# Interleaving two attention groups in one unit order, with the query rotations and norm spreads as side steps between the units

## The reference, cut to what matters

```python
# A: latent attention, causal, one rotated key shared by the heads
q_nope = rmsnorm(q[..., :64], g_qn);  q_rope = rope(rmsnorm(q[..., 64:], g_qr), pos)
s = (q_nope @ k_nope.T + q_rope @ k_rope.T) * scale          # p, o as usual
# B: sliding windows (128,1), (512,4), (2048,16), merged by their softmax denominators
s = (qs @ ks.T) * 64**-0.5                                    # with the windows' mask
# new tokens: the same two, against 16 pages of 128 cached latents (A)
# and the last rows of a window buffer (B), for each of 8 sequences
h = h + concat(rmsnorm(o_a, g_oa), rmsnorm(o_b, g_ob)) @ w_o
h = h + (silu(f @ w_gate) * (f @ w_up)) @ w_down
y = h + sigmoid(rmsnorm(h, g_ple) @ w_ple_gate + b) * (p @ w_ple_proj)
```

## Time and profile before

| | |
|---|---|
| median of 3 runs | 1137.56 us (1137.51 to 1141.03) |
| the profiled execution's own time | 1142.85 us |
| its span, from the first to the last instruction | 1140.9 us |
| PE busy | 1104.0 us, 97% of the span |
| DVE busy | 572.8 us, 50% |
| ACT busy | 468.1 us, 41% |
| mean granted TensorE clock | 0.982 of full speed |

### The profile page before, as it was taken

The page is one execution under the profiler, slowest core; times in us unless marked ns, Lnnn a source line. Parts: engine busy times, 40 slices in busy tenths (PEclk is TensorE's granted clock), DMA queues, the critical chain, the costliest instruction groups (busy, mean ns, idle before and its releaser), DMA issues.

```text
span 1140.9 us, 21284 instructions
## 1 busy us (share of the span) xinstructions
PE 1104.0 (97%) x8198; PEld 952.6 (83%) x8198; DVE 572.8 (50%) x998; ACT 468.1 (41%) x812; POOL 84.7 (7%) x124
## 2 busy tenths in 40 slices
PE   6999999989989999999998999999999999999998
PEld 6997888545657777777766999999999999999997
DVE  4221344276367566676655995344323343444644
ACT  4334322356356656565565344333221232223432
POOL 5300011060000000000000130000000000000000
PEclk9999999989799999999998999999999999999999
DMA  7763642239457677788851245645723554652222
GB/s 273 256 220 132 222 134 61 77 135 327 173 177 247 188 247 249 250 266 265 257 164 38 76 147 185 222 164 169 266 90 138 185 202 165 220 189 92 70 77 93
DMA packets 68589, 202.79 MB, mean 178 GB/s; under 512 B 7425, under 2 KB 40194, under 8 KB 67234
## 3 DMA queue, kind: packets, MB, share of 16 engines
q1 hardware_dynamic: 66338, 131.89, 35.2%
q0 software_dynamic: 2176, 69.90, 17.4%
HBM read 196.67 MB, written 72.13 MB: 236 GB/s over the span
## 4 chain that ended last, share of the span: by engine, by line
PE 88%; DVE 5%; ACT 3%; issue 2%; DMA 2%; POOL 0%; SPq 0%; DVEq 0%; ACTq 0%
PE ps L548 53%; PE ps L1309 14%; PE ps L1412 4%; DMA kv<-in_wkt 1%; PE ps L1286 1%; PE ps L1297 1%; PE ps L1366 1%; PE ps L1341 1%; PE ps L1360 1%; PE ps L448 1%; PE ps L485 1%; PE ps L476 1%; PE ps L1276 1%; PE ps L1183 1%; PE ps L1271 1%
## 5 line engine op out<-in xcount | busy, mean ns | idle before, releaser
L548 PE MATMUL ps<-aHi,wHi 128*128 128x272 f32 x1168 | 247.3, 293 | 10.7 <-DVE wLo L427 8.9
L548 PE MATMUL ps<-aHi,wLo 128*128 128x272 f32 x1168 | 242.8, 289 | 0.0
L548 PE MATMUL ps<-aLo,wHi 128*128 128x272 f32 x1168 | 242.2, 289 | 0.0
L427 DVE TENSOR_TENSOR wLo<-ring,wHi 128x1024 fp32r<-128x1024 f32 (+3 forms) x103 | 142.6, 1384 | 142.0 <-ACT wHi L422 141.8
L422 ACT ACTIVATE wHi<-ring 128x1024 fp32r<-128x1024 f32 (+3 forms) x103 | 114.4, 1111 | 240.4 <-PE ps L548 209.2
L548 PEld LDWEIGHTS ps<-aHi,wHi 128*128 128x128 f32 x1168 | 185.1, 190 | 19.0 <-DVE wLo L427 11.2
L548 PEld LDWEIGHTS ps<-aLo,wHi 128*128 128x128 f32 x1168 | 185.0, 190 | 0.0
L548 PEld LDWEIGHTS ps<-aHi,wLo 128*128 128x128 f32 x1168 | 183.7, 190 | 0.0
L1625 DVE TENSOR_REDUCE ssq<-att 128x8 f32<-128x512 f32 x128 | 87.2, 681 | 83.4 <-ACT att L899 83.4
L899 ACT ACTIVATE att<-ps 128x512 f32<-128x512 f32 x128 | 76.4, 597 | 106.8 <-PE ps L1309 106.3
L1309 PE MATMUL ps<-wkHi,pgHi 128*128 128x512 f32 x256 | 104.2, 407 | 1.5 <-DVE pgLo L1619 1.2
(11 more groups left out here) (259 smaller groups left out, 1480.3 us busy)
## 6 DMA issues: line engine op xcount, KB each, us to landing
out_o_cv<-in_cv POOLq DMA_DIRECT2D x16, 2044.0 KB, 9.4
ring<-in_wgu SPq DMA_DIRECT2D x44, 512.0 KB, 4.1
big<-in_pgt SPq DMA_DIRECT2D x128, 144.0 KB, 2.2
big<-in_pgl SPq DMA_DIRECT2D x128, 128.0 KB, 2.4
kv<-in_ck SPq DMA_DIRECT2D x8, 1792.0 KB, 10.4
ring<-in_win SPq DMA_DIRECT2D x21, 512.0 KB, 4.0
kv<-in_cv SPq DMA_DIRECT2D x8, 1024.0 KB, 5.6
kv<-in_cv SPq DMA_DIRECT2D x24, 256.0 KB, 6.3
```

The source lines that it names most:

```text
L427: nc.vector.tensor_tensor(wLo[:, u % 2, 0:width], ring[:, u % 2, 0:width], wHi[:, u % 2, 0:width].bitcast(F32), ALU.subtract).then_inc(w_l ...
L548: ins = nc.tensor.matmul(pair[rows, a, 0:HT], w[:, c], xx[:, k, a * HT:(a + 1) * HT], start=(k == 0 and z == 0), stop=(k == nk - 1 and z = ...
```

## The change

The units begin with three B units; then A and B units alternate until B runs out. The two rotations and the four spreads of the A queries become side steps of the loop, each with a place of its own in the alternation of the score pairs, ahead of units 1 and 2 (rotations) and 3, 5, 7 and 9 (spreads). A's first block of a pair waits for that pair's own scaled and rotated queries. The loop's first scores wait only for the values' copies. `wkT` moves to another room and is loaded right after the queries. SP then waits for all scores, and issues the remaining pages and the 16 latents of the first sequence, and only then the window keys; the first sequence's window scores move from page 7 to page 12. Four of the eight output squares move into the last sequence's pages, two more ahead of its exponentials, and the root's table and first root move behind the new tokens' copies. In `ple` the gate product has a semaphore of its own, on which DVE's first multiply waits.

```diff
-        wkT = kv2[:, 2048:2048 + HP * KVL].rearrange("p (c n) -> p c n", c=HP)
+        wkT = kv1[:, 2048:2048 + HP * KVL].rearrange("p (c n) -> p c n", c=HP)
...
-        units = [(p, i) for p in (4, 5, 6, 7, 0, 1, 2, 3) for i in range(4)]
+        LEAD = 3
+        units_a = [(p, i) for p in range(HP) for i in range(4)]
+        units_b = [(p + HP, i) for p, i in units_a]
+        units = units_b[:LEAD]
+        for k in range(len(units_a)):
+            units += [units_a[k]] + units_b[LEAD + k:LEAD + k + 1]
...
+        QR_AT, QN_AT = (1, 2), (3, 5, 7, 9)
+        SIDE_AT = QR_AT + QN_AT + (ABSORB, NEW)
...
         def place(u):
-            return u + (u >= ABSORB) + (u >= NEW)
+            return u + sum(u >= at for at in SIDE_AT)
+
+        def side_place(at):
+            return at + SIDE_AT.index(at)
...
-        WIN_AT = 7
+        def win_at(b):
+            return 7 if b else 12
...
             sp.wait_ge(w_used, W_QB + NQT)
+            sp.dma_start(wkT, wkt).then_inc(s_wkt, 16)
             load_pages(0, range(11))
-            sp.wait_ge(a_pv, 2 * H)
+            sp.wait_ge(a_s, 2 * len(units))
             sp.wait_ge(out_s, 80)
-            sp.dma_start(wkT, wkt).then_inc(s_wkt, 16)
             sp.wait_ge(p_new, 1)
+            sp.wait_ge(p_nw, 1)
+            load_pages(0, range(11, NPG))
             load_latent(0)
             sp.wait_ge(a_pv, 4 * H)
             load_win_k(0)
+            load_pages(1, range(RING - NPG))
             sp.wait_ge(a_o, H)
-            sp.wait_ge(out_s, 80)
-            sp.wait_ge(p_nw, 1)
-            load_pages(0, range(11, NPG))
-            load_pages(1, range(RING - NPG))
             load_win_v(0)
...
+                    if b == NB - 1 and t - 11 in range(4):
+                        out_square(t - 11)
...
-            for k in range(4):
+            for k in range(4, 6):
                 out_square(k)
...
-            for k in range(4, KD):
+            for k in range(6, KD):
                 out_square(k)
-            sqrt_table()
...
-            out_root(0)
             act.wait_ge(ou_g, 1)
...
+            sqrt_table()
+            out_root(0)
             out_root(1)
...
-            pe.wait_ge(v_ev, 4)
-            pe_rot(g_qr[0])
-            pe_spread(g_qn[0])
-            pe_rot(g_qr[1])
-            pe_spread(g_qn[1])
-            pe.wait_ge(n_out, out_no[g_qn[0]])
-            pe_spread(g_qn[2])
-            pe.wait_ge(n_out, out_no[g_qn[1]])
-            pe_spread(g_qn[3])
-
-            pe.wait_ge(n_rope, len(turning))
-            pe.wait_ge(n_out, out_no[g_qn[3]])
...
             for n in range(len(units) + LAG_PV):
+                if n in QR_AT:
+                    score_room(side_place(n))
+                    pe_rot(g_qr[QR_AT.index(n)])
+                if n in QN_AT:
+                    score_room(side_place(n))
+                    pe_spread(g_qn[QN_AT.index(n)])
...
+                        if i == 0:
+                            pe.wait_ge(n_out, out_no[g_qn[p]])
+                            pe.wait_ge(n_rope, rope_no[g_qr[2 * p // HP]])
...
-            for k in range(2):
+            for k in range(4):
                 out_sum(k)
             row_max(NB - 1)
-            for k in range(2, 4):
+            for k in range(4, 6):
                 out_sum(k)
...
-                    for k in range(HP, KD):
+                    for k in range(6, KD):
                         out_sum(k)
...
-                mm3(W_PL + j, P, ps[2 * j], FULL, a_split, i=m * 2, step=step)
+                gate = mm3(W_PL + j, P, ps[2 * j], FULL, a_split, i=m * 2, step=step)
...
+                gate.then_inc(pl_gate, 1)
...
             for n in range(len(units) + LAG_PV + 1):
+                if n in QR_AT:
+                    dve_rope(g_qr[QR_AT.index(n)])
+                if n in QN_AT:
+                    dve_scale(g_qn[QN_AT.index(n)])
...
-                v.wait_ge(w_used, m + (W_PL + j + 1))
+                v.wait_ge(pl_gate, m + (j + 1))
...
                 v.wait_ge(pl_act, m + (j + 1))
+                v.wait_ge(w_used, m + (W_PL + j + 1))
```

More of the change, by code:

```diff
@@ L319, in spread_pair @@
         def spread_pair(g):
-            return ps[3 - g_qn.index(g) % 2] if g in g_qn else ps[2] if g == g_qr[1] else ps[3]
+            return score_pair(side_place(QN_AT[g_qn.index(g)])) if g in g_qn else ps[2] if g == g_qr[1] else ps[3]
         def rot_pair(g):
-            return ps[g_qr.index(g)] if g in g_qr else ps[3]
+            return score_pair(side_place(QR_AT[g_qr.index(g)])) if g in g_qr else ps[3]
         def row_of(g):
@@ L565, in sp_weight_loop @@
                     sp_weight(u0 + j, pairs[j, bass.ds(f, 1), :, :].rearrange("a p n -> p (a n)"), f * 2)
-        units = [(p, i) for p in (4, 5, 6, 7, 0, 1, 2, 3) for i in range(4)]
+        LEAD = 3
[4 more added lines that the diff above has]
+            units += [units_a[k]] + units_b[LEAD + k:LEAD + k + 1]
+        rounds_done = [u for u in units if u[1] == 3]
         NEGM, SUM, REC1 = range(3)
@@ L918, in scaled, with out_square @@
                 act.activation(On[:, KVL:], ps[3][:, 1, :], ACT.Copy, scale=rec[:, 1:2]).then_inc(m_on, 1)
+            def out_square(k):
+                if k == 2:
+                    act.wait_ge(w_sc, NB)
+                if k >= 4:
+                    act.wait_ge(ou_sum, k - 3)
+                act.activation(square_of(k), aT[:, k, 0:NP_], ACT.Square).then_inc(ou_sq, 1)
             act_tail = {4: exps, 5: win_exps, 9: scaled}
@@ L1204, in _ @@
             pe_spread(g_qr[1])
-            pe.wait_ge(v_ev, 4)
-            pe_rot(g_qr[0])
-            pe_spread(g_qn[0])
-            pe_rot(g_qr[1])
-            pe_spread(g_qn[1])
-            pe.wait_ge(n_out, out_no[g_qn[0]])
-            pe_spread(g_qn[2])
-            pe.wait_ge(n_out, out_no[g_qn[1]])
-            pe_spread(g_qn[3])
-            pe.wait_ge(n_rope, len(turning))
-            pe.wait_ge(n_out, out_no[g_qn[3]])
-            def score_room(x):
-                if x < 2:
-                    return
-                if x - 2 == A_PLACE:
+            def score_room(x):
+                sides = [side_place(at) for at in SIDE_AT]
+                if x == 0:
+                    pe.wait_ge(v_ev, 4)
+                elif x == 1:
+                    pe.wait_ge(n_out, out_no[g_qr[0]])
+                elif x - 2 in sides[:2]:
+                    pe.wait_ge(n_rr, rope_no[g_qr[sides.index(x - 2)]])
+                elif x - 2 in sides[2:6]:
+                    pe.wait_ge(n_out, out_no[g_qn[sides.index(x - 2) - 2]])
+                elif x - 2 == A_PLACE:
                     pe.wait_ge(p_all, 1)
@@ L1291, in _ @@
                     pe.wait_ge(a_tc, m + 1)
-                    if i == 0 and m >= 8:
-                        pe.wait_ge(a_o, m // 4 - 1)
+                    if i == 0 and p % HP:
+                        pe.wait_ge(a_o, rounds_done.index((p - 1, 3)) + 1)
                     for j in range(i + 1):
@@ L1296, in _ @@
                             h = 2 * p + z
-                            last = mm(ps[2][z * HD:(z + 1) * HD, m // 4 % 2, i * P:(i + 1) * P],
+                            last = mm(ps[2][z * HD:(z + 1) * HD, p // HP, i * P:(i + 1) * P],
                                       (vA if p < HP else vB)[:, j, (h % H) * HD:(h % H + 1) * HD],
@@ L1548, in _ @@
             dve_recip(P_QH)
+            v.wait_ge(kn_sq, 1)
+            v.tensor_reduce(rkN[:, :], tmp[0:NS, 1, 0:512].rearrange("p (h d) -> p h d", h=H), AX.X, ALU.add).then_inc(kn_ss, 1)
             dve_scale(g_qr[0])
             dve_scale(g_qr[1])
-            v.wait_ge(kn_sq, 1)
-            v.tensor_reduce(rkN[:, :], tmp[0:NS, 1, 0:512].rearrange("p (h d) -> p h d", h=H), AX.X, ALU.add).then_inc(kn_ss, 1)
             v.wait_ge(k_rt, 1)
             link(v.reciprocal(rkN[:, :], rkN[:, :]))
-            dve_rope(g_qr[0])
-            dve_scale(g_qn[0])
-            dve_rope(g_qr[1])
-            for g in g_qn[1:]:
-                dve_scale(g)
             for n in range(len(units) + LAG_PV + 1):
+                if n in QR_AT:
+                    dve_rope(g_qr[QR_AT.index(n)])
+                if n in QN_AT:
+                    dve_scale(g_qn[QN_AT.index(n)])
                 if n == ABSORB:
```

16 lines of the change are left out of this document (5 added, 11 removed).

## The result

| | before | after |
|---|---|---|
| median, compared run by run | 1138.80 us (1137.51 to 1141.03, 4 runs) | 1127.32 us (1126.12 to 1128.57, 4 runs) |
| the profiled execution's own time | 1142.85 us | 1126.12 us |
| its span | 1140.9 us | 1124.3 us |
| mean granted TensorE clock | 0.982 | 0.992 |

The ratio is 0.9897, with a 95% interval of 0.9874 to 0.9920.

A forecast was written before the change was run, and what follows sets the result against it. PE bounds the kernel (88% of the chain), so gaps, low clock and work standing alone can be won. Terms sum to -11.5 us on the profiled 1142.85, giving 1131.4; shifted by 5.3 to the median, 1126.1, range 1119.5 to 1133.5.

The forecast's parts named there:

- The loop's start and the other spreads: Start of prompt attention: earlier fifth unit but later clock rise, -1.5 us; three spreads moved into PE's stream, +1.9.
- The alternation: Prompt attention loop: alternating A and B units cuts PE's gaps from 6.0 to 2.0 us, -4.0, bounds -6 and 0.
- all others are covered: Alternation's gap count: apart from gaps after A's 4-block and 2-block units, PE's work covers DVE's time.
- rival (2): Prompt attention: PE was the bound and the alternation only moves its gaps; -7.5 us in all, 1130.1; chance 0.08.
- `wkT` early and the clock at `absorb`: At `absorb`: PE's wait for the load goes, -1.2 us; half clock behind it goes partly, -3.0 from 0 to -6.1.
- The first sequence's loads: First pages: window keys land at 25 us, PE needs them at 25.5; +0.3 us, bounds 0 and +4.
- Rival (3): First sequence's window scores at page 12: keys come late, PE waits 10 us, low clock +5; 1138 to 1142; chance 0.07.
- The way into the output projection: Last page to output projection: earlier PE start and two sums fewer of four, together -2.5 us.
- `ple`: Last `ple` unit: first multiply and sigmoid start when the gate is done, 12 matmuls earlier; -1.5 us.
- rival (1): Clock drops at `absorb` anyway or was up in the median run, start stays low longer; -5.0 us, 1132.6; chance 0.15.
- (4): Prompt attention from 225 us: alternating scores and spreads keep PE at half clock; slower by clock alone; chance 0.05.
- (5): Output projection and `ple`: the two ends bring nothing as another wait takes over; -7.5 us, 1130.1; chance 0.05.

The follow-up runs named there:

- e9: The changed kernel itself, unaltered, run again on another chip beside three variants: 1126.78 us, ratio 0.9919 to before.
- e5: The changed kernel with rotations and spreads ahead of the loop again, alternation kept: 1129.14 us, ratio 0.9945 to before.
- e11: The changed kernel with the first B pair's 4-block unit put ahead of A's first unit: 1128.84 us, ratio 0.9932 to before.
- e1: The kernel before with only `wkT` in its other room and loaded ahead of the pages: 1133.21 us against 1134.15, ratio 0.9991.
- e10: The changed kernel without the alternation, all B units then all A units: 1127.08 us, ratio 0.9923 to before.
- e2: The kernel before with only the gate's own semaphore in the last stage: 1132.45 us, ratio 0.9978 to before.
- e3: The kernel before with only the early squares, later root and moved sums at the output projection: 1130.93 us, ratio 0.9972 to before.
- e6: The changed kernel with the first sequence's window scores at page 7 again instead of 12: 1133.82 us, ratio 0.9989 to before.
- e12: The changed kernel with e11's exchange of two units and the new tokens' scores one step later: 1123.76 us, ratio 0.9906 to before.
- e8: The changed kernel with `wkT`'s load held until 23 units have their scores: 1146.88 us, ratio 1.0108 to before.

## Why the prediction was right

The time was right, and the ends of the kernel were right in their mechanism and near in size; inside the loop the terms were off in opposite directions. That the median was met within 1.2 us is in part luck: the sum was worked out for the profiled execution, where it was 5.1 us short, and on the chip of e9 the same change is worth 6.9 us.

**The loop's start and the other spreads** (-1.5 and +1.9, so +0.4): the fifth unit's scores start at 236.36 (236.34 in e9) instead of the forecast 238.0 and the 241.00 of before, so -4.6 where -3.0 was forecast, and the transposes at 238.17 take 0.87 us, their time at full clock, so the clock is up from there and not from 242.7. That is the early-clock bound (-4.5). The mis-sized steps are "all at half clock" and "some 4 us later": of the 17.7 us at half clock that the prediction implies (225 to 242.7) 7.0 were there, 10.7 x 0.38 = 4.1 us better. In this execution the rotations between B's scores ran at the higher level (1.16 and 1.18 us); in e9 they did not (1.81 and 1.60). The DVE-late gap at A's first unit was named, but 2.46 us long and not 0.8: DVE scales the first A queries, for which the unit waits, only behind the masks of the third unit and the scaling of the second:

```profile
232.37 0.77 DVE L520 SCALAR_TENSOR_TENSOR aT<-aT,G,ps 128x544 f32<-128x544 f32 x1
```

The other spreads were near their price (0.73 us each for 0.64). But POOL's layout of the new queries, which now comes behind the last of them, stands beside a scaling of DVE that takes 1.42 us at 254.87, where the same shape took 0.62 at 243.99, and PE waits 1.02 us for it at 256.35. In e5, where POOL has done this layout earlier, that scaling takes 0.62 and the gap is 0.22. That POOL's work is what slows DVE is not shown by a run of its own. In all the side steps measured -1.96 (e5 to after by the stretch), or -0.32 with e9's execution, for +0.4.

**The alternation** (-4.0): the formula's gaps were right, the sum was not. Forecast were 0.4 and 0.2 us a round; 0.37, 0.37, 0.21 and 0.37 were there, and 1.02 for the 0.2 of the first round. But the step "all others are covered" failed where DVE's 3.1 us for the new tokens come between a 4-block unit's masks and its scaling (2.15 where the sum has nothing), and the first A unit's wait belongs to this order too, since e11 takes most of it away by the order alone. Of the 4.0, 1.5 is left between e1 and e5 by the stretch, and nothing that can be told between e9 and e10. So rival (2), "the alternation only moves its gaps", is what the runs fit best, by a way that it did not name. (That the formula "gives the observed 0.57 exactly" was no test of it: the 2.36 us were read to PE's start, so 2.36 - 1.79 is that gap by definition.)

**`wkT` early and the clock at `absorb`** (-1.2 and -3.0): in the profiled execution both were there in full (-7.41), in the time of e1 at most 2.4 us. The prediction's reservation ("this stretch need not be in each of them") was right, and its half price lies between the two; in how many executions the stretch is there, no profile shows beyond the four of the old loop (one with it, three without). The sum was taken on an execution 5.3 us above the median and then shifted by those 5.3; that it came out right rests on half of this stretch being priced, and on the other misses. The Trainium skill, TensorE: Matmul & The Clock Gate, Part 1, "What's actually happening", has activity lift the clock; the fuller stream of the changed kernel agrees with it in the profile after (1.00 from 245 to 330), less in e9 (0.83 over 305 to 315), and e2 and e3 keep 1.00 at `absorb` with the old order as well. What they lack is the wait.

**The first sequence's loads** (+0.3): from the first page to the projection 274.13 us, and 273.95 in e3, which has the squares but the old loads: +0.2. The window keys went out 14.3 us after the last scores (319.4 to 333.71; forecast 14 to 15) and PE came to them at 344.67 without a wait. Rival (3), late keys, was 1 us away; e6 shows what it costs.

**The way into the output projection** (-2.5): -3.77 in the profiles with the loads' +0.3, -4.1 between e1 and e3, -3.2 in e3's time. The mechanism was right: PE itself is last at 602.23, two sums are left of four (1.80 for 3.52), and 1.2 us are won ahead of it where 0.8 was forecast. Most of the rest is the first product, at 5.17 us for 5.78 and 4.20 in e3; the granted clock over 600 to 640 us is 0.92 for 0.87.

**`ple`** (-1.5): -1.47 in the profiles, 1.50 in e2's timeline.

Summed over the profiled executions, the forecast -11.5 stands against -16.6: the absorb stretch with its wait 3.2 more, the start and its spreads 2.4 more, the way with the loads 1.6 more, the alternation 2.5 less, and 0.5 that belongs to no edit (0.14 ahead of the first spreads, 0.39 from there to `absorb` between before and e1, where the loop is the same). Of rival (1) the half holds that before has no low clock at `absorb` in other executions (e2, e3), but the start of the changed kernel is low for a shorter time, not a longer one. Rivals (4) and (5) did not come about: no half clock from 245 to the first page in the profile after, 3.4 us in e9's, and both ends paid. The argument against rival (4), that the A part before runs at 1.00 throughout, misread its row: one of that part's stretches is at 0.66. And two figures do not follow from their own terms: the lower bound of 1119.5 comes to 1121.5 (3.1 and half of 3.0 off 1126.1), and 0.88 less a tenth is 0.79, not 0.83. Neither moves the forecast.

What stays open: the single runs of one kernel spread widely (e11 from 1122.99 to 1129.94, e12 from 1119.81 to 1129.02), more than the gaps that e11 and e12 close. They go with the clock: the fastest of e12 has a mean granted clock of 0.997 and the slowest 0.987, in e11 it is 0.995 and 0.988. In which stage an execution loses it, one profile each doesn't show. Half clock behind a short wait, present in one profile and absent in another, is a candidate that was seen (e9 against after, at the same gap), not a shown cause. Nor do the times tell what the side steps alone are worth.

## What to carry to other kernels

A low-clock stretch behind a short wait is a property of one execution until a second profile shows it too: price it, but look at how far that execution lies from the median before pricing it whole. Compare two profiles over the stretch that an edit touches, and know how far two profiles of one kernel differ there (2.2 us here). When two streams are interleaved to cover an engine's latency, cost the odd steps too: the first unit of the second stream, and whatever the other engine does once between a unit's scores and its scaling. Work that must be done anyway (here rotations and spreads) can serve as filler in a stretch that would otherwise wait; here it left less half clock at the start of the stage in every profile, and a gain in time that is not clear of the spread.

## What the runs showed of the hardware that was not expected

- The same program point runs at either clock level in different executions. The rotation of four 128x272 matmuls behind the first spreads took 2.15 us in before, 1.81 in e1 and 1.16 in e3 with the same instructions ahead of it on PE, and 1.16 in after and 1.81 in e9, which are one kernel; `absorb` took 3.61 us in before, 1.98 in e2, whose loop is the same.
- The same gap of 2.15 us is followed by half clock in one execution of the changed kernel (transposes of 1.97 us in e9) and by full clock in another (1.09 us).
- A load from SP's queue among POOL's value copies took 16.3 us in before, 14.9 in e2 and 5.8 in e3, with the same loop, enough to turn a hidden load into a wait in one of them; held back in e8, it took 21.3.
- A scaling on DVE took 1.42 us in after where its shape takes 0.62, and 2.15 in e10 where its shape takes 0.48, each while POOL ran its two memsets of 128x1024 (254.04 to 255.87, and 252.35 to 254.19).
